# Weight sums of the seven-product panels on GpSimd instead of VectorE, in a hybrid decoder layer pair

## The reference

```python
def mixing_block(x, st, l, P, lb, pos0):
    proj = jnp.einsum('btd,de->bte', x, P['w_in'][l]).astype(jnp.float32)
    ...
    ya, h1, buf1 = rglru_group(xa, ga, h0, buf0, ...)
    yb, c1, n1, m1 = mlstm_group(qb, kb, vb, ob, ib, fb, c0, n0, m0, ...)
    yc, sr1 = retention_group(qc, kc, vc, gc, sr0, f('ret_norm_g'), pos0)
    yd, sh1 = hgrn2_group(qd, fd, id_, gd, sh0, lb, f('hgrn_norm_g'))
    mixed = jnp.concatenate([ya, yb, yc, yd], axis=-1).astype(x.dtype)
    out = jnp.einsum('bte,ed->btd', mixed, P['w_out'][l])
    return out, (h1, buf1, c1, n1, m1, sr1, sh1)
```

## Time and profile before

| | |
|---|---|
| time, median of 3 runs | 1004.39 us (1003.72 to 1005.49) |
| span of the profiled execution, first to last instruction | 1002.8 us |
| PE busy | 986.8 us, 98% of the span |
| DVE busy | 504.6 us, 50% |
| ACT busy | 193.0 us, 19% |
| POOL busy | 81.8 us, 8% |
| mixing of layer 0, about 25 to 155 us | PE busy 129.6 of 130 us, DVE 111.0 |
| mixing of layer 1, about 440 to 585 us | PE busy 144.2 of 145 us, DVE 121.6 |

### The profile page before, as it was taken

One profiled execution on the slowest core, in us unless ns is written; L12 is line 12 of the kernel. 1 busy time (PEld: TensorE's weight loads), 2 busy tenths in 40 slices (PEclk: granted clock), 3 DMA queues, 4 the chain that ended last, 5 costly groups with the idle time before them and its releaser, 6 DMA issues.

```text
span 1002.8 us, 23772 instructions
## 1 busy us (share of the span) xinstructions
PE 986.8 (98%) x10688; PEld 789.7 (79%) x10688; DVE 504.6 (50%) x1032; ACT 193.0 (19%) x414; POOL 81.8 (8%) x105
## 2 busy tenths in 40 slices
PE   9999999999999999999999999999999999999995
PEld 6897877999999999998988779556666767667533
DVE  6888894764666654269878975430101201011135
ACT  1333333221111000044333241400000000000001
POOL 1110021600000000000000200230000020000020
PEclk9999999999999999999999999999999999999998
DMA  9427349214443155201233378899999999999982
GB/s 356 148 90 240 117 151 368 91 74 180 168 168 128 74 191 222 108 29 57 86 103 132 120 307 333 332 331 379 402 415 398 422 391 412 425 421 423 422 334 83
DMA packets 37498, 241.43 MB, mean 241 GB/s; under 512 B 5008, under 2 KB 8144, under 8 KB 17680
## 3 DMA queue, kind: packets, MB, share of 16 engines
q1 hardware_dynamic: 27280, 216.69, 55.3%
q0 software_dynamic: 6432, 19.43, 5.4%
q10 hardware_dynamic: 3680, 3.74, 1.2%
HBM read 228.60 MB, written 13.07 MB: 241 GB/s over the span
## 4 chain that ended last, share of the span: by engine, by line
PE 91%; DVE 4%; DMA 3%; ACT 1%; issue 1%; SPq 0%; DVEq 0%
PE ps L773 69%; PE ps L1378 15%; PE ps L1486 6%; DMA up_slots<-in_moe_w 3%; PE ps L776 1%; PE ps L1315 1%; DVE overlay L2506 0%; DVE small L2459 0%; ACT up_slots L1835 0%; ACT x L1835 0%; DVE tables L3096 0%; DVE x L2266 0%; ACT overlay L1835 0%; DVE overlay L2261 0%; DVE overlay L2464 0%
## 5 line engine op out<-in xcount | busy, mean ns | idle before, releaser
L773 PE MATMUL ps<-up_slots,mix_or_moe 128*32 128x352 f32 (+2 forms) x3248 | 238.8, 451 | 0.6 <-DMA up_slots<-in_moe_w 0.4
L773 PEld LDWEIGHTS ps<-up_slots,mix_or_moe 128*32 128x32 f32 (+2 forms) x3248 | 135.5, 111 | 96.3 <-issue 9.3
L773 PE MATMUL ps<-x,up_slots 128*128 128x144 f32 (+3 forms) x832 | 152.3, 336 | 0.0
L773 PEld LDWEIGHTS ps<-x,up_slots 128*128 128x128 f32 x832 | 124.7, 190 | 25.1 <-issue 8.8
L773 PE MATMUL ps<-overlay,tables 128*32 128x256 f32 (+4 forms) x1992 | 121.5, 375 | 0.0
L773 PEld LDWEIGHTS ps<-overlay,tables 128*32 128x32 f32 (+2 forms) x1992 | 91.6, 113 | 26.6 <-issue 2.4
L3135 DVE TENSOR_TENSOR mix_or_moe<-mix_or_moe,ps 128x352 f32<-128x352 f32 x24 | 11.2, 518 | 174.0 <-PE ps L773 174.0
L1378 PE MATMUL ps<-overlay,up_slots 128*128 128x144 f32 x704 | 91.7, 286 | 0.6 <-DVE overlay L2911 0.3
L1378 PEld LDWEIGHTS ps<-overlay,up_slots 128*128 128x128 f32 x704 | 88.3, 190 | 1.1 <-issue 0.8
L773 PE MATMUL ps<-up_slots 128*128 128x144 f32 (+2 forms) x768 | 87.1, 282 | 1.2 <-DVE up_slots L2540 1.0
L773 PEld LDWEIGHTS ps<-up_slots 128*128 128x128 f32 (+2 forms) x768 | 79.5, 186 | 5.3 <-DVE up_slots L2540 1.9
(11 more groups left out here) (379 smaller groups left out, 1010.5 us busy)
## 6 DMA issues: line engine op xcount, KB each, us to landing
up_slots<-in_moe_w SPq DMA_DIRECT2D x64, 1408.0 KB, 24.9
overlay<-in_moe_w SPq DMA_DIRECT2D x21, 1536.0 KB, 26.7
up_slots<-in_ffn_w SPq DMA_DIRECT2D x30, 1024.0 KB, 6.9
up_slots<-in_w_in SPq DMA_DIRECT2D x27, 1024.0 KB, 5.1
up_slots<-in_w_out SPq DMA_DIRECT2D x8, 1024.0 KB, 7.3
overlay<-in_moe_w SPq DMA_DIRECT2D x7, 1024.0 KB, 26.4
mix_or_moe<-in_states POOLq DMA_DIRECT2D x6, 512.0 KB, 7.3
expert_tokens<-in_shape_tables POOLq DMA_DIRECT2D x8, 384.0 KB, 7.6
```

Source lines behind the costliest of these rows:

```text
L773: return pe.matmul(o, lhsT, rhs, start=start, stop=stop)
```

## The change

The four sums of each panel leave DVE's program and stand in POOL's, with the same operands, the same order and the same counting semaphore, so that PE's waits are the same as before. In POOL's program the sums of panels 0 to 2 stand ahead of the first masked copy, those of panels 3 to 6 behind it (in layer 0 behind the eight DMAs too), and those of panel 7 behind the third masked copy and ahead of the stores. `BLOCKS`, `loaded` and `seven_sum` are unchanged, and so are the programs of PE, ACT and SP.

```diff
@@ in POOL's program, after pool.memset(ATALL, 0.0) @@
+                def panel_sums(q):
+                    w11, w12, w22, w21, s2, s4, s1 = BLOCKS[SEVEN_BUF[q]]
+                    pool.wait_ge(S[f"sx_in_{SEVEN_BUF[q]}"], loaded["seven", l, q])
+                    pool.tensor_tensor(s1, w21, w22, ALU.add).then_inc(S["sx_w"], 1)
+                    pool.wait_ge(*seven_sum(l, q, 0))
+                    pool.tensor_tensor(s2, s1, w11, ALU.add).then_inc(S["sx_w"], 1)
+                    pool.tensor_tensor(w21, w21, w11, ALU.add).then_inc(S["sx_w"], 1)
+                    pool.wait_ge(*seven_sum(l, q, 1))
+                    pool.tensor_tensor(s4, s2, w12, ALU.add).then_inc(S["sx_w"], 1)
...
+                for q in range(3):
+                    panel_sums(q)
                 pool.wait_ge(*mark("ml_ac", "vt", l))
                 values(VM_ML, 0)
                 if l == 0:
                     for e in range(NE):
                         pool.dma_start(XG[CAP * e:CAP * e + CAP, :], tab[0:CAP, 0:D]).then_inc(S["xg_zeroed"], 16)
+                for q in range(3, 7):
+                    panel_sums(q)
                 pool.wait_ge(*mark("lru_dv", "out", l))
                 pool.wait_ge(*mark("hg_ac", "vt", l))
                 values(VM_HG, 2)
                 pool.wait_ge(*mark("ret_ac", "vt", l))
                 pool.wait_ge(*mark("ml_dv", "rr", l))
                 values(VM_RET, 1)
+                panel_sums(7)
@@ in DVE's program @@
-                def panel_sums(q, steps=(0, 1, 2, 3)):
...
                 boundary(4)
-                panel_sums(0)
-                panel_sums(1)
                 operands(3)
...
                 boundary(6)
-                panel_sums(2)
                 operands(5)
...
                 panel_outputs(2)
-                panel_sums(3)
                 lru_decay()
...
                 head_scale(6, Y_ML, "mlstm_norm_g", "ml_dv")
-                panel_sums(6, (0, 1))
                 panel_outputs(5)
-                panel_sums(6, (2, 3))
...
                 gelu_in()
-                panel_sums(7)
```

More of the change, by code:

```diff
@@ L2708, in mix @@
                 mlstm_pstate()
-                panel_sums(4, (0, 1))
                 mlstm_states()
-                panel_sums(4, (2, 3))
                 merge(7, 2)
@@ L2722, in mix @@
                 weights(6, 1, "ret_dv", "w23")
-                panel_sums(5)
                 need("hg_ps", "keys")
```

## The result

| | before | after |
|---|---|---|
| time, median (range), 4 runs each | 1004.22 us (1003.72 to 1005.49) | 1021.86 us (1020.46 to 1022.77) |
| ratio, 95% interval | | 1.0170 (1.0156 to 1.0184) |
| span of the profiled execution | 1002.8 us | 1020.6 us |

The account below looks back on a forecast made before the run. PE, busy 98%, was taken to bound the kernel, so freeing DVE gains 0; stalls of 2.9 + 1.3 + 1.8 + 1.3 = 7.3 us on the 1002.8 span, plus 1.6 to the median, give 1011.7 us, range 1006.7 to 1016.5.

Parts of the forecast that it names:

- hidden after all: Rival: DVE's instructions beside the sums lose no more than its lead, so not slower, 1004.4 us; chance 0.09.
- late in each mixing: Rival: panel 7's sums and last masked copies delay panel 5's outputs, up to 2 us per layer, 1015.7; chance 0.09.
- POOL's first add starts late: Rival: start-up cost moves panel 0's sums onto `gate_maxima()`, 3.6 instead of 2.9 us; over 12 us, no cost; chance 0.08.
- PE's clock falls in a stall: Rival: clock goes to 1.2 GHz at the two stalls above 1.5 us, 4.7 us more, 1016.4; chance 0.04.
- four stalls: PE waits for DVE's delayed work at panels 0 and 2 of both layers: 2.9, 1.3, 1.8 and 1.3 us.
- Level 4: Panel 2's sums during `conv()` make DVE's operands 2.5 us late, margin 1.47: stall 1.3 us in each layer.
- The walk: Step-by-step timing of POOL's sums and DVE's blocked instructions taking turns; in the conv, three pairs fit between four adds.
- the first term: Layer 0, panel 0: 2.9 us with copies taken as blocked; 0.4 us smaller without them blocked.
- level 0 of layer 0: Panel 0's sums make DVE's operands 3.35 us late, margin 0.45: PE stalls 2.9 us, bounds 0 to 3.6.
- Layer 1, 1.8 forecast: Panel 0's sums delay DVE's token sums, gate and `forget()`, no margin: stall of 1.3 to 2.2 us, taken as 1.8.

Follow-up runs that it names:

- e1: The changed kernel with the sums of panels 0 to 2 of each layer back on DVE at their old places: 1004.98 us, ratio 1.0003.
- e8: The kernel before with only panel 0's sums on POOL, in both layers: 1012.21 us, ratio 1.0095.
- e9: The kernel before with only panel 2's sums on POOL, in both layers: 1013.02 us, ratio 1.0099.
- e10: The changed kernel with panel 2's sums waiting until DVE has made the conv's first scalar_tensor_tensor: 1019.10 us, ratio 1.0160.
- e5: The kernel before, sums on DVE, plus four useless POOL memsets of 128 x 1408 at each of the four places: 1017.40 us, ratio 1.0123.
- e2: The changed kernel, all sums on POOL, with three waits that move sums of panels 0 to 2 behind level operands: 1006.60 us, ratio 1.0023.
- e4: The kernel before, sums on DVE, plus four useless POOL adds of 128 x 512 at each of the four places: 1019.44 us, ratio 1.0148.
- e6: The kernel before with useless DVE adds ahead of the operands of levels 0 and 4, nothing on POOL: 1017.18 us, ratio 1.0128.

## Why the prediction was wrong

**What held.** PE bounds the kernel, and the removed 44 us are worth nothing (e1). The place of each loss: panels 0 and 2 in both layers (e8, e9), none for panels 3 to 7 (e1), and none for panel 1, during whose sums in after, layer 0, DVE stood idle for 7.81 us behind an exponential of ACT. POOL and DVE exclude each other and take turns (after, e10). The sums are never late for PE. Of the rivals, "hidden after all", "late in each mixing" and "POOL's first add starts late" did not come: no stall in the last third, and the first sum stood 0.03 us behind the memset.

**The step that failed: "PE's clock falls in a stall, 0.04".** The forecast made four stalls, two of them above 1.5 us by its own figures, and left the clock at 1.00 because "no mixing row shows it". It could not: no stall above 0.5 us was there. The same trace did show a fall, outside the mixings, where PE has little left to do (a row of PE, and the window behind it with the clock at 0.50):

```profile
994.42 0.38 PE L773 MATMUL ps<-small,tables 128*128 128x1 f32 x2 [1.64 <-ACT overlay L1835]
996.00:998.00 2.00, 0.00 (x0) 0.00 (x0) 1.93 (x5) 0.00 (x0) 0.00 (x0) 0.50 0.30 119
```

It didn't tell how short a stall suffices, but it was no ground for 0.04. Four stalls above 1.5 us came, three cost the clock, 4.9 us. That the rival's price, 4.7 us, is near is luck: it counted two falls as long as their stalls, 2.9 and 1.8 us, where three of 1.6 to 1.7 us came, one of them at a stall that was forecast as 1.3. With it the forecast would have been 1016.4, the edge of the range.

**Mis-sized terms.** The stalls sum to 9.8 us, not 7.3. Of the 10.2 us by which the forecast was short, the clock is 4.9 and the stalls are 2.5; the other 2.8 lie outside what the forecast summed, most of them, by after's profile, behind the mixings. The stalls:
- Level 4, twice 1.3 forecast, 2.41 and 2.42 measured. The walk started the sums of panel 2 ahead of the six L2361 and took what stands before them, copies and L2359, as free, so that the first sum cost nothing. After and e5 show both held up. The Trainium skill's page that I named, "SBUF — State Buffer", says so for copies and for tensor_scalar ("Who interferes with whom"); the sum used it for copies in the first term, and not for this one.
- The walk also let pairs of DVE's instructions through between two sums. In e10, where only the six count, the group is 3.81 us longer, three sums of 1.27 us. At level 0 of layer 0 the delay is 3.27 + 0.45 = 3.7 us, at level 4 it is 2.41 + 1.47 = 3.9. Four sums in a row held DVE up for about three of them in all three places, with either kind of blocked instruction.
- Level 0 of layer 0, 2.9 forecast, 3.27 measured, within its bound of 3.6. A sum takes 1.26 to 1.28 us where nothing disturbs it, above the 1.15 that I took and above both rows that I took it from (1.04 and 1.18). Layer 1, 1.8 forecast, 1.7 measured.

## What to carry to other kernels

Before work goes to GpSimd, ask not whether VectorE has too much to do but what VectorE has to deliver while GpSimd works: count every VectorE instruction there that has two SBUF operands or is a copy or tensor_scalar within SBUF, and take the GpSimd time less one instruction as the delay (four sums cost about three here). Where TensorE is near 100% busy, price each new stall with the clock that may fall behind it, 1.6 us and up to 3.3 here. The same sums placed a few microseconds later (e2) lost 2 us instead of 17.6.

## What the runs showed of the hardware

**When a stall costs the clock.** New stalls ahead of level 0 and level 4 in the profiles of after and e4 to e10:

| stall | clock fell to 0.5 behind it |
|---|---|
| 2.51 to 3.38 us | 10 of 10 |
| 1.66 to 2.49 us | 7 of 12 |
| 1.06 to 1.50 us | 0 of 5 |

The same place with 2.42 us came out both ways within e9. One fall stands outside the table: in e5 the clock fell between 44 and 45 us, behind a wait of 0.47 us and eighteen matmuls of four columns, while stalls of 0.25 to 0.48 elsewhere cost nothing. What decides it I leave open.

**What a memset on GpSimd blocks.** Copies and tensor_scalar within SBUF, even a copy of 128 x 64, and nothing with two operands (e5).

**Not settled.** Why four sums cost three and not four, why after loses 2.9 us more than e4 with the same stalls and falls, and what makes e6 2 us longer than its stalls and its clock.
